# Output projection in three rounded products by halves, the gates of a mixture of single-neuron experts sent in pieces, and the prompt's choice in two parts, on one Trainium2 core

## The reference

```python
q, k, v, f = split_in(h, w_in[l])          # h = rmsnorm(x) * (1 + sc1) + sh1
att = diff_attention(q, k, v, lam)         # 4 heads, two softmax maps each
four = fourier_mix(f, w_fourier[l])        # FFT over positions and channels, per-group map
x = x + g1 * mixer_merge(att, four, subln_g[l], lam_init, w_out[l])   # concat @ w_out
h2 = rmsnorm(x) * (1 + sc2) + sh2
x = x + g2 * peer(h2, w_query[l], sub_keys[l], expert_u[l], expert_v[l])
y = rmsnorm(x, final_g)

def peer(h, w_query, sub_keys, expert_u, expert_v):   # 128*128 experts of one neuron
    q = (hf @ w_query).reshape(T, 8, 2, 128)
    s = jnp.einsum('thpk,hpnk->thpn', q, sub_keys)
    s1, i1 = lax.top_k(s[:, :, 0], 16); s2, i2 = lax.top_k(s[:, :, 1], 16)
    ...                                    # the 16 best sums of the pairs, per head
    g = jax.nn.softmax(top_s)              # 8 heads x 16 gates for each token
    a = gelu(einsum('tkd,td->tk', expert_u[ix], hx))
    return einsum('tk,tkd->td', gx * a, expert_v[ix])
```

## Time and profile before

| | before |
|---|---|
| median of 3 executions | 1820.45 us (1818.86, 1820.45, 1822.13) |
| profiled execution | 1815.94 us, span 1813.9, mean granted clock of TensorE 0.966 |
| busy share of the span | PE 92%, PEld 79%, DVE 83%, ACT 36%, POOL 51% |
| chain that ended last | PE 79%, DVE 10%, DMA 5%, issue 3%, ACT 3% |
| stages (us from the start) | output projection from 311, queries from 386, gate tables to about 707, experts from 719, last sums at 1785 |

### The profile page before, as it was taken

One profiled execution on the slowest core, in us unless ns is written; L12 is line 12 of the kernel. 1 busy time (PEld: TensorE's weight loads), 2 busy tenths in 40 slices (PEclk: granted clock), 3 DMA queues, 4 the chain that ended last, 5 costly groups with the idle time before them and its releaser, 6 DMA issues.

```text
span 1813.9 us, 28223 instructions
## 1 busy us (share of the span) xinstructions
PE 1665.3 (92%) x9322; PEld 1442.0 (79%) x9338; DVE 1506.1 (83%) x3069; ACT 645.6 (36%) x1085; POOL 916.1 (51%) x771
## 2 busy tenths in 40 slices
PE   4999998999954886899999999999999999999994
PEld 2776766479953886799999999999999999999993
DVE  0732266457999999799999999999999999999997
ACT  1212266121103785233333333333333333333331
POOL 1101000013402665777778877777666666666661
PEclk9999999999976998999999999999999999999997
DMA  9445202140010668999999999999999999999993
GB/s 355 173 163 208 75 1 98 42 184 3 1 47 1 187 186 253 385 406 409 407 408 390 402 409 409 409 409 409 409 408 409 409 409 403 410 409 407 406 397 124
DMA packets 198137, 518.28 MB, mean 286 GB/s; under 512 B 14643, under 2 KB 64435, under 8 KB 197941
## 3 DMA queue, kind: packets, MB, share of 16 engines
q0 software_dynamic: 73728, 268.47, 37.3%
q1 hardware_dynamic: 122320, 245.59, 36.3%
q10 hardware_dynamic: 2022, 3.38, 0.5%
HBM read 486.45 MB, written 30.93 MB: 285 GB/s over the span
## 4 chain that ended last, share of the span: by engine, by line
PE 79%; DVE 10%; DMA 5%; issue 3%; ACT 3%; POOL 0%; SPq 0%; POOLq 0%; ACTq 0%; DVEq 0%; PEldq 0%; another core or an unknown queue 0%
PE ps L1786 20%; PE ps L1785 20%; PE ps L1784 19%; PE ps L1758 4%; PE ps L1873 4%; DMA arena_w<-in_w_mod 2%; PE ps L1599 2%; PE ps L1603 2%; PE ps L1600 2%; PE ps L1697 2%; DMA arena_w<-in_w_in 1%; ACT arena_w L867 1%; DVE arena L1470 1%; PE ps L1721 1%; DVE arena L1307 1%
## 5 line engine op out<-in xcount | busy, mean ns | idle before, releaser
L1786 PE MATMUL ps<-hT_hi,U_lo 128*128 128x384 f32 x1024 | 344.3, 336 | 0.0
L1784 PE MATMUL ps<-hT_hi,U_hi 128*128 128x384 f32 x1024 | 344.1, 336 | 0.0
L1785 PE MATMUL ps<-hT_lo,U_hi 128*128 128x384 f32 x1024 | 343.5, 335 | 0.0
L537 POOL DMA_INDIRECT rows_under<-in_expert_u,idxn x192 | 273.8, 1426 | 116.4 <-issue 41.8
L1784 PE MATMUL ps<-hT_hi,C_hi 128*128 128x512 f32 x768 | 301.2, 392 | 14.5 <-DVE C_lo L1447 14.5
L537 POOL DMA_INDIRECT rows_under<-in_expert_v,idxn x192 | 242.7, 1264 | 140.4 <-DVE arena L1470 77.8
L1786 PE MATMUL ps<-hT_hi,C_lo 128*128 128x512 f32 x768 | 303.2, 395 | 0.0
L1785 PE MATMUL ps<-hT_lo,C_hi 128*128 128x512 f32 x768 | 303.1, 395 | 0.0
L1470 DVE SCALAR_TENSOR_TENSOR arena<-rows_under,dots,arena 128x1024 f32<-128x1024 f32 x192 | 247.8, 1291 | 4.8
L930 ACT ACTIVATE act_t<-ps 128x384 f32<-128x384 f32 x128 | 63.0, 492 | 386.2 <-PE ps L1786 386.2
L1784 PEld LDWEIGHTS ps<-hT_hi,U_hi 128*128 128x128 f32 x1024 | 192.6, 188 | 4.9
(11 more groups left out here) (273 smaller groups left out, 3010.9 us busy)
## 6 DMA issues: line engine op xcount, KB each, us to landing
U_in<-in_expert_uT SPq DMA_DIRECT2D x128, 512.0 KB, 8.7
arena<-in_expert_v SPq DMA_DIRECT2D x128, 512.0 KB, 6.5
arena_w<-in_w_mod SPq DMA_DIRECT2D x12, 2048.0 KB, 12.4
gate_in<-gates_scratch SPq DMA_DIRECT2D x62, 384.0 KB, 7.9
gates_scratch<-arena_w SPq DMA_DIRECT2D x5, 4096.0 KB, 16.6
arena_w<-in_w_in SPq DMA_DIRECT2D x4, 2048.0 KB, 8.7
arena_w<-in_w_query SPq DMA_DIRECT2D x4, 2048.0 KB, 10.8
arena_w<-in_w_out SPq DMA_DIRECT2D x2, 2048.0 KB, 8.4
```

Source lines behind the costliest of these rows:

```text
L537: pool.indirect_dma_start(out=rowr[row], out_offset=None, in_=table, in_offset=bass.IndirectOffsetOnAxis(ap=idxn[:, g, row:row + 1], axis= ...
L1784: nc.tensor.matmul(out, hi, rhi, start=start, stop=False)
L1785: nc.tensor.matmul(out, hi, rlo, start=False, stop=False)
L1786: return nc.tensor.matmul(out, lo, rhi, start=False, stop=stop)
```

## The change

1. **Output projection.** Both operands are split into a rounded part and a rest: ACT's `mix_out` and `att_out` now write `mix_hi`, DVE's new `mix_low` and `att_low` write `mix_lo` from the same banks; ACT's `out_high` and POOL's `out_low` split the weights. `merge` runs `products3`, so a half is 24 matmuls. All first halves come first, into sums of their own (`half_sum`), then each second half with the transpose of the block before. `query_low(0)` moves from DVE to POOL; the first query weights come later and to another place.
2. **Gates.** `GCUT` has steps of 8 pairs. Only the first part (512 KB) is sent before the loop; parts 1 to 7 leave from SP's loop at the turns in `SENT`. The reads of x move to the turns in `BACK`.
3. **Choice.** `choose` is parted: `candidates(4)` and the first lookup ahead of the loop, the second lookup and the weights inside its first expert block, ahead of row 2.
4. **Gathers.** Row 2 of the first eight waits for the first gate pair only.

The diff, cut to its core:

```diff
-GCUT = (0, 8, PAIRS)
+GCUT = tuple(range(0, PAIRS + 1, 8))
+SENT = {1: 2, 2: 4, 3: 6, 4: 8, 5: 12, 6: 15, 7: 18}
+BACK = {0: 9, 1: 11, 2: 14, 3: 17, 4: 20, NBLK: 23}
...
+        mix_hi = HT_lo
...
+        wo_hi = [w_lo[:, DFT_C % WRING], wq_lo_first[:, :, :]]
+        wo_lo = [w_lo[:, (OUT_C + half) % WRING] for half in range(OUT_CH)]
...
@@ SP
-            sp.wait_ge(s_mix, NBLK)
             sp.wait_ge(s_out, 32)
+            sp.wait_ge(s_fill2, NBLK)
             sp.dma_start(wq_in[0], w_query_v[:, :, 0:NC]).then_inc(s_wq[0], 16)
...
-                    for r in range(len(GCUT) - 1):
-                        pairs = slice(GCUT[r], GCUT[r + 1])
-                        sp.dma_start(to[:, pairs], held[:, pairs]).then_inc(s_gpart[r], 16)
+                    sp.dma_start(to[:, 0:GCUT[1]], held[:, 0:GCUT[1]]).then_inc(s_gpart[0], 16)
...
+            turn = 1
+            for at in sorted(set(SENT.values()) | set(BACK.values())) + [TWICE]:
+                for r in range(1, len(GCUT) - 1):
+                    if turn < 4 * r < at:
+                        load_pairs(turn, 4 * r)
+                        turn = 4 * r
+                    if turn == 4 * r:
+                        sp.wait_ge(s_gpart[r], 16)
+                load_pairs(turn, at)
+                turn = at
+                for r in SENT:
+                    if SENT[r] == at:
+                        send_part(r)
...
@@ POOL
+            out_low(0)
             for b in range(NBLK):
                 pool.wait_ge(s_avar, b + 1)
                 pool.tensor_tensor(ss4[:, 1, :], ss4[:, 0, :], powe[:, 0:H], ALU.pow).then_inc(s_arstd, 1)
+            out_low(1)
             for b in range(NBLK):
+                if b == NBLK - 1:
+                    query_low(0, range(2 * b - 2, 2 * b))
                 pool.wait_ge(s_var2, b + 1)
                 pool.tensor_tensor(rstd[:, b:b + 1], ss[:, b:b + 1], powe[:, 0:1], ALU.pow).then_inc(s_rstd2, 1)
+                if 0 < b < NBLK - 1:
+                    query_low(0, range(2 * b - 2, 2 * b))
...
                 if first and row == 2:
-                    for part in s_gin:
-                        pool.wait_ge(part, 16)
+                    pool.wait_ge(s_gin[0], 16)
...
@@ ACT
-                    act.copy(mixT[:, 4 + g, 0:P], src[:, 0:P]).then_inc(s_act1, 1)
+                    act.copy(mix_hi[:, 4 + g, 0:P], src[:, 0:P]).then_inc(s_fhi, 1)
...
+                if i < KD // 2:
+                    out_high(0, range(2 * i, 2 * i + 2))
+            out_high(1, range(KD))
...
@@ DVE
+                if i:
+                    mix_low(units[i - 1])
...
+                if i % H == 2 and i > 2 * H:
+                    att_low(i // H - 2)
...
+            for b in range(NBLK):
+                merge(b, 0)
+            for b in range(NBLK):
+                merge(b, 1)
+                var2(b)
+                if b:
+                    turned_low(b - 1)
+                make_h2(b)
+            turned_low(NBLK - 1)
...
-            choose(4, 0, 0, 0, (0, 0))
+            candidates(4, 0, 0)
+            picked(4, (0,))
+
+            def first_row(i, q):
+
+                if i == 0 and q == 2:
+                    picked(4, (1,))
+                    gate_weights(4)
+                dot_row(0)(i, q)
...
@@ PE
-                    pe.wait_ge(s_mix, b)
+                    pe.wait_ge(s_mixlo, b)
...
                 for k in range(KD):
-                    last = nc.tensor.matmul(out, mixT[:, k, b * P:(b + 1) * P], chunk[:, (OUT_C + half) % WRING, k, :],
-                                            start=(k == 0), stop=(k == KD - 1))
+                    if b == 0:
+                        pe.wait_ge(s_olo, KD * half + k + 1)
+                    last = products3(out, mix_hi[:, k, b * P:(b + 1) * P], mix_lo[:, b, k, :],
+                                     wo_hi[half][:, k, :], wo_lo[half][:, k, :], k == 0, k == KD - 1)
                 last.then_inc(s_fill2, 1)
...
+            for b in range(NBLK):
+                merge(b, 0)
+            for b in range(NBLK):
+                merge(b, 1)
+                if b:
+                    turned(b - 1)
```

More of the change, by code:

```diff
@@ L95, in _phase1_jobs @@
         if i:
-            jobs.append((("fmix",) + units[i - 1], "act"))
-    jobs.append((("fmix",) + units[-1], "act"))
+            jobs.append((("fmix",) + units[i - 1], "dve"))
+    jobs.append((("fmix",) + units[-1], "dve"))
     return jobs
 def _phase2_jobs():
-    order = ["m0", "m1", "m2", "T0", "m3", "T1", ("merge", 4, 0), "T2", ("merge", 4, 1), "T3", "T4"]
-    jobs = []
-    for o in order:
-        if isinstance(o, tuple):
-            jobs.append((o, "dve"))
-        else:
-            kind = "merge" if o[0] == "m" else "h2T"
-            jobs += [((kind, int(o[1]), half), "dve") for half in range(2)]
+    jobs = [(("merge", b, 0), "dve") for b in range(NBLK)]
+    for b in range(NBLK):
+        jobs.append((("merge", b, 1), "dve"))
+        jobs += [(("h2T", b - 1, half), "dve") for half in range(2 if b else 0)]
+    jobs += [(("h2T", NBLK - 1, half), "dve") for half in range(2)]
     return jobs
@@ L506, in _, with out_low, query_low @@
             pool.wait_ge(s_bc, 4 * MOD_CH)
+            def out_low(half):
+                src = chunk[:, (OUT_C + half) % WRING]
+                for k in range(KD):
+                    pool.wait_ge(s_ohi, KD * half + k + 1)
+                    pool.tensor_tensor(wo_lo[half][:, k, :], src[:, k, :], wo_hi[half][:, k, :].bitcast(f32),
+                                       ALU.subtract).then_inc(s_olo, 1)
+            def query_low(ci, ks):
+                for k in ks:
+                    pool.wait_ge(s_qhi, KD * ci + k + 1)
+                    pool.tensor_tensor(wq_lo[ci][:, k, :], wq_in[ci][:, k, :], wq_hi[ci][:, k, :].bitcast(f32),
+                                       ALU.subtract).then_inc(s_qlop, 1)
+            out_low(0)
             for b in range(NBLK):
@@ L1120, in _ @@
                     dve.tensor_copy(fstage[:, i % 2, 1, 0:P], src[:, 0:P]).then_inc(s_dve1, 1)
+                if i:
+                    mix_low(units[i - 1])
+            mix_low(units[-1])
             dve.wait_ge(s_lam, 1)
@@ L1156, in att_norm, with att_low @@
                 dve.tensor_tensor(a, a, ss4[:, 1, :].unsqueeze(2).broadcast_to([P, H, P]), ALU.mult).then_inc(s_att, 1)
+            def att_low(b):
+                dve.wait_ge(s_mix, b + 1)
+                dve.scalar_tensor_tensor(out=mix_lo[:, b, 0:4, :], in0=ps[:, 7, :].rearrange("p (h t) -> p h t", h=H),
+                                         scalar=lam[:, 7:8], in1=mix_hi[:, 0:4, b * P:(b + 1) * P].bitcast(f32),
+                                         op0=ALU.mult, op1=ALU.subtract).then_inc(s_mixlo, 1)
             neg_max(0)
-            for i in range(len(UNITS) + 5):
+            for i in range(len(UNITS) + 7):
                 if i < len(UNITS):
@@ L1346, in select, with picked @@
                     dve.wait_ge(s_selfill, min(n, NDEN))
-                for w in range(2):
+            def picked(n, ws, bd=0, share=(0, 0, 0, 0)):
+                b = ORDER[n]
+                for w in ws:
                     gate_quads(bd, share[2 * w])
@@ L1358, in select @@
                                            spread(onehot[:, 1]), ALU.add))
+                if ws[-1] == 0:
+                    return
                 if n < NDEN:
```

174 lines of the change are left out of this document (83 added, 91 removed).

## The result

The changed kernel takes **1841.21 us** in the median of 4 runs (1838.78 to 1845.60), the kernel before 1819.65 in 4 runs beside it: a ratio of 1.0125, 95% interval 1.011 to 1.014, so 22 us slower. Forecast were 1812.7 us and a range of 1805 to 1821. The profiled execution took 1842.94 us, its span is 1841.1.

A forecast was written before the change was run, and what follows sets the result against it. TensorE was busy 92% of the span, but no one bound covered the program, so it went by stage. Projection -6.2, entry -5.5 and loop +4.0 sum to -7.7 us: 1820.45 to 1812.7 us, range 1805 to 1821.

The forecast's parts named there:

- The send's price: Expert loop: seven 512 KB gate sends at 1.81 us each, with the x1 reads, cost +4 us (bounds 0 and +9).
- the ring: Expert loop: the ring of eight gathered rows absorbs some 3 of the 9 us by which extra transfers exceed the slack.
- The rival of a dearer loop: Expert loop: sends cost 7 us and the first gate multiply does not move, giving 1818.8 us; chance 0.19.
- three signs of being wrong: Attention DVE passes a microsecond longer beside POOL, gates landing no sooner, or PE idle over 8 us inside the loop.
- the rival that the engines have room: Expert loop: sends cost nothing, giving 1808.8 us, or 1806.8 with an attention cheaper by 2; chance 0.27.
- So POOL waits, and DVE loses 0.13 us a time: Attention and second halves: POOL waits when both read SBUF; DVE held by POOL costs +0.3 us in all.
- Rival 1: POOL holds DVE for whole passes, 10.2 us in the attention plus 5.1 in the second halves, giving 1828; chance 0.07.
- The projection, -6.2 net: Output projection: three rounded products start the queries 10.4 us sooner, less 4.2 us of costs ahead of it.
- A block takes 7.1 us on DVE: Projection's second halves: DVE needs 7.1 us a block against 5.44 + 0.87 on PE, so DVE sets the pace.
- +4.2: Costs ahead of the projection, in Fourier stage and attention, with DVE held by POOL: +4.2 us (bounds +1 and +8).
- A start of the queries that is x earlier makes the loop x earlier: Between projection and loop entry, up to 707 us, the order of work is kept, so the queries' gain carries over whole.
- The entry, -5.5: Loop entry: first gate multiply 3.0 us earlier, another 2.5 from rows and choice; -5.5 us (bounds -2.5 and -7.5).

The follow-up runs named there:

- e2_window: Changed kernel with all gates sent ahead of the loop and POOL's `query_low(0)` passes moved behind h2 and the next sum: 1811.17 us, ratio 0.9960.

## Why the prediction was wrong

**The send's price, the step that failed.** "A send costs 0.524 MB / 290 = 1.81 us" and "+4 us (bounds 0 ... and +9)": the loop lost 31 us, from -3.6 to +27.4. The bytes alone were priced about rightly: seven copies in rows of 4 KB cost 7 us (9 by the ratios), at the upper end of the bounds. What was missing is the packet. The 290 GB/s came from a send with the engines to itself, where its 512-byte pieces did no harm; in the loop the same pieces stand beside the 4 KB rows of the gathers (11.9 to 16.5 us to land), and the send sits in SP's queue ahead of U. The forecast let POOL's gathers be late, by the ring and the landing of rows. They stayed on time (DVE waited 2.8 us for them from 740 to 1400); U was late, with no ring behind it. The rival of a dearer loop went the right way and had 7 us; no rival had this one. What would have shown it ahead: the shape of the DMA in the code (a row of 128 floats for each pair and partition) and the queue that it enters, with the question what stands right behind it. The prediction named three signs of being wrong, and all came: passes of DVE beside POOL that are a microsecond longer, a first piece of the gates that lands no sooner, and PE idle over 8 us in the loop (20.6).

The Trainium skill, "DMA: Bandwidth & Descriptors", section "Queues, rings and completion order", says that an engine goes round between the queues that have work, a packet at a time. The runs agree, if packet is what the profile counts: beside 4 KB rows on q0 the sends and copies in 512-byte pieces took 10.3 to 16.5 us to land and the copies in 4 KB rows 8.5 to 8.9. Its section "Where 436 GB/s comes from" was put behind the rival that the engines have room. That rival is ruled out: seven 4 KB copies should then have cost nothing.

**POOL's ports, the rival that had 0.07.** "So POOL waits, and DVE loses 0.13 us a time" rested on one line of POOL and five DVE passes of the gate stage, and did not carry over: here POOL's pass begins first (239.00 against 239.06, 364.14 against 364.29), and DVE is held. Rival 1 said 10.2 us for the attention and 5.1 for the second halves. Measured: 4.3 (in the traces) and 4.6. As a mechanism it was right. It took the projection's gain; the 22 us on top came from the sends. The Trainium skill's page "SBUF — State Buffer", section "Who interferes with whom", which speaks against such a change, is borne out in each point that these runs touch: DVE's pass with two SBUF operands waits for POOL's whole instruction (0.35 to 1.26 us, and L1280 0.69 to 1.25), a pass with one operand in PSUM does not (L1278 0.69). The rows of one stage, where POOL was the one that waited, were too little to set it aside.

**The projection, -6.2 net.** A half took 5.44 us as priced (the DVE sums of the first halves are 5.44 apart). "A block takes 7.1 us on DVE" measured 7.3 once POOL was out of the way, 8.65 with it. The stretch from the merges to the first query: forecast 11.2 shorter (74.8 to 63.6; 10.4 seen from query 2), measured 7.2 with POOL in the way and 11.6 without (`e2_window`). Ahead of it +4.2 was forecast; measured in the means +4.7 up to the last unit and +1.2 behind it, with 4.3 of that from POOL. The query's start in the mean of six traces with POOL's passes unmoved is 385.3 (382.6 to 390.9) against 386.5 (385.9 to 387.8) of before's code: -1.2 instead of -6.2, within the scatter. With both of POOL's passes moved it is 378.8 (377.4 to 380.3), -7.7. So the ports account for the shortfall.

**"A start of the queries that is x earlier makes the loop x earlier"** held while the gain was small and lost 3 of 7.7 us once it was real.

**The entry, -5.5.** The send to `C_lo` shrank by 4.6 us. The piece by itself did not land in 4.4 us but in 6.2 (708.84 to 715.03), no sooner than with 3.5 MB behind it (5.6 before, 5.2 to 7.2 over all twelve such traces); the reading back took 3.3 instead of 6.0. Together the gates are 2.1 us sooner, where 3.0 were forecast. Of the 2.5 us for rows and choice all is the single wait, none the parting, since DVE was waiting for the gates anyway.

Sum by these measures, against before: -1 for the projection, -4.6 for the entry, +31 in the loop, about +25, where the medians are 22 apart. The two profiled executions are 27 apart; between them the queries start 1.1 us later, which gives 27.5.

## What to carry to other kernels

- A DMA is priced by its packets and by its queue, not by its bytes: ask how long each contiguous piece is, and what critical load stands behind it in the same queue. Here 3.5 MB cost 25 us in 512-byte pieces in SP's queue, 7 to 9 there in 4 KB rows, and some 5 in 512-byte pieces in ACT's queue.
- When work moves to POOL, list the DVE passes beside it that read all their operands from SBUF (here those with two tensors, and a TENSOR_SCALAR with one). A wait that places POOL's pass beside PSUM reads, or where DVE waits, gave back 4.6 us here.
- Work taken off DVE ahead of a wait of DVE's own is worth nothing, however neatly it is placed later.

## What the runs showed of the hardware that was not expected

- Where POOL and DVE alternate on two-operand SBUF passes, both stretch: h2's passes 1.3 to 2.2 us, POOL's pair 2.53 to 3.50. Even a 128x1 product on DVE (L1207) took 1.03 us instead of 0.16 beside POOL.
- The same attention code took 63.1, 64.1 and 67.2 us in three executions. The granted clock from 230 to 262 us was 0.89, 0.84 and 0.68 in them. Yet their first queries start at 385.9, 387.8 and 385.9 us, since the last Fourier copy stood 4 us earlier in the third. It was not tried what sets either.
- From the send of the first 512 KB of gates to the reading back took 6.2 and 6.9 us in the two traces with nothing sent behind it, and 5.2 to 7.2 us in the twelve with 3.5 MB behind it: taking these away did not make it land sooner.
- The same 512-byte sends took 20.3 to 20.7 us to land from ACT's queue and 11.9 to 16.5 from SP's.
